# Two transformer blocks on one core: the FFNs' normed input made in three stages over three pairs of panels, and the split buffers at three distances mod 512 from the moving tiles

## The reference

```python
def rmsnorm(x, gain):
    y = xf * lax.rsqrt(jnp.mean(xf * xf, axis=-1, keepdims=True) + NORM_EPS_2)
    return (y * gain.astype(jnp.float32)).astype(x.dtype)

def modulate(h, shift, scale):
    return h * (1.0 + scale) + shift

def swiglu(u, wg, wu, wd):
    return (jax.nn.silu(u @ wg) * (u @ wu)) @ wd

    # in each layer l; the second FFN in the same way with mod 6, 7 and 8
    u = modulate(rmsnorm(h, norm_ffn1[l]), mod[:, :, 0], mod[:, :, 1])
    h = h + 0.5 * (1.0 + mod[:, :, 2]) * swiglu(u, ffn1_wg[l], ffn1_wu[l], ffn1_wd[l])
```

## Time and profile before

| | us |
|---|---|
| median of 3 runs | 1980.22 |
| lowest and highest | 1978.51 and 1980.4 |
| the profiled execution's own time | 1979.45 |
| its span, first to last instruction | 1978.1 |
| TensorE matmul busy | 1879.3 (95%) |
| VectorE busy | 1352.3 (68%) |
| ScalarE busy | 955.4 (48%) |
| DMA engines, mean rate | 197 GB/s |

### The profile page before, as it was taken

The page is one execution under the profiler, slowest core; times in us unless marked ns, Lnnn a source line. Parts: engine busy times, 40 slices in busy tenths (PEclk is TensorE's granted clock), DMA queues, the critical chain, the costliest instruction groups (busy, mean ns, idle before and its releaser), DMA issues.

```text
span 1978.1 us, 34269 instructions
## 1 busy us (share of the span) xinstructions
PE 1879.3 (95%) x15080; PEld 1811.9 (92%) x15080; DVE 1352.3 (68%) x1831; ACT 955.4 (48%) x1320; POOL 62.3 (3%) x76
## 2 busy tenths in 40 slices
PE   7998988899999888999999999999999999999998
PEld 7987988899788887999989899999999999799998
DVE  5666676665766767777676857777777776856555
ACT  5564554455645545444455335345434456344443
POOL 0000100000001000000000000001000000010000
PEclk9998999989989998999999999999999999999999
DMA  7453446463443554566545344665666456345551
GB/s 305 173 198 130 185 184 226 184 240 144 186 179 139 222 212 179 226 246 243 218 184 236 117 168 181 248 253 236 235 239 248 193 195 237 125 149 192 177 186 65
DMA packets 59285, 389.71 MB, mean 197 GB/s; under 512 B 6656, under 2 KB 9472, under 8 KB 15232
## 3 DMA queue, kind: packets, MB, share of 16 engines
q1 hardware_dynamic: 59136, 387.52, 51.1%
HBM read 386.45 MB, written 1.05 MB: 196 GB/s over the span
## 4 chain that ended last, share of the span: by engine, by line
PE 67%; DVE 21%; ACT 10%; issue 1%; DMA 0%; POOL 0%; SPq 0%; DVEq 0%; ACTq 0%
PE banks L757 17%; PE banks L758 16%; PE banks L759 16%; DVE weights_split L905 7%; ACT weights_split L899 4%; PE bank L758 4%; PE bank L757 4%; PE bank L759 4%; ACT map L1340 2%; DVE weights L885 1%; DVE xbc L2311 1%; DVE map_stat L1528 1%; ACT map L1346 1%; PE bank L825 1%; PE bank L838 1%
## 5 line engine op out<-in xcount | busy, mean ns | idle before, releaser
L905 DVE TENSOR_TENSOR weights_split<-weights,weights_split 128x2048 fp32r<-128x2048 f32 (+2 forms) x306 | 657.1, 2149 | 320.1 <-ACT weights_split L899 319.4
L757 PE MATMUL banks<-u,weights_split 128*128 128x258 f32 (+2 forms) x2032 | 583.3, 287 | 20.2 <-DVE weights_split L905 11.4
L899 ACT CAST weights_split<-weights 128x2048 fp32r<-128x2048 f32 (+2 forms) x306 | 542.9, 1776 | 77.0 <-PE bank L759 45.2
L758 PE MATMUL banks<-u,weights_split 128*128 128x258 f32 (+2 forms) x2032 | 577.8, 284 | 0.0
L759 PE MATMUL banks<-u,weights_split 128*128 128x258 f32 (+2 forms) x2032 | 577.7, 284 | 0.0
L757 PEld LDWEIGHTS banks<-u,weights_split 128*128 128x128 f32 (+1 forms) x2032 | 389.3, 192 | 24.7 <-DVE weights_split L905 12.4
L758 PEld LDWEIGHTS banks<-u,weights_split 128*128 128x128 f32 (+1 forms) x2032 | 389.2, 192 | 0.4
L759 PEld LDWEIGHTS banks<-u,weights_split 128*128 128x128 f32 (+1 forms) x2032 | 388.7, 191 | 0.4
L757 PE MATMUL banks<-x,weights_split 128*128 128x256 f32 x1056 | 302.4, 286 | 15.0 <-DVE weights_split L905 10.0
L758 PE MATMUL banks<-x,weights_split 128*128 128x256 f32 x1056 | 296.7, 281 | 0.0
L759 PE MATMUL banks<-x,weights_split 128*128 128x256 f32 x1056 | 296.6, 281 | 0.0
(11 more groups left out here) (320 smaller groups left out, 2519.6 us busy)
## 6 DMA issues: line engine op xcount, KB each, us to landing
weights<-in_weights SPq DMA_DIRECT2D x262, 1024.0 KB, 6.9
weights<-in_ada SPq DMA_DIRECT2D x80, 1024.0 KB, 4.8
weights<-in_weights SPq DMA_DIRECT2D x36, 512.0 KB, 5.4
weights<-in_weights SPq DMA_DIRECT2D x4, 576.0 KB, 5.3
constants_second<-in_constants_second SPq DMA_DIRECT2D x1, 1792.0 KB, 9.3
weights<-in_weights SPq DMA_DIRECT2D x2, 640.0 KB, 7.4
h<-in_x SPq DMA_DIRECT2D x2, 512.0 KB, 5.2
out<-xbc SPq DMA_DIRECT2D x4, 256.0 KB, 2.1
```

The costliest lines, as they stand in the source:

```text
L757: pe.matmul(out, left[0], right[0], start=start, stop=False, **more)
L758: pe.matmul(out, left[0], right[1], start=False, stop=False, **more)
L899: act.do.copy(split[:, 0, 0:n], raw[:, 0:n]).then_inc(*self.act_wrote.inc(("weights", key)))
L905: dve.do.tensor_tensor(split[:, 1, 0:n], raw[:, 0:n], split[:, 0, 0:n].bitcast(F32), ALU.subtract).then_inc(*self.dve_wrote.inc(("weights" ...
```

## The change

Pairs 0, 1 and 2 of each FFN (`RAWS = 3`) still use the raw input, which has a tile `raw` of its own now, with rows of 258 words. Meanwhile the normed input is made in `u`, whose rows are now 256 words: VectorE scales h by coefficient and factors into `squares`, ScalarE adds the shift and casts the high part into `u`, VectorE writes the low part. The step `normed` is issued six times, three times in pair 1 and three times in pair 2. At turn t VectorE scales chunks 2t and 2t+1, ScalarE makes the high parts of the two chunks before these, and VectorE the low parts of the two before those. Pairs 3 to 10 use `u`: 256 columns, one Silu of 512 wide from the bank on ScalarE, one multiplication of 512 wide from the bank on VectorE, with no scaling and no shift column. The modulations begin at pair 3 instead of pair 1. A spacer of 32 words stands behind each of the three split buffers instead of behind the last. Waits for the reuse of the raw tile and the factors name the third pair of the FFN before instead of its last.

```diff
@@ -60,13 +60,13 @@
...
 PAIRS = FC // 2
+RAWS = 3
 PLACES = HIDDEN_BLOCKS // 2
...
 SPLIT_SLOTS = 3
-U_ROW = 384
 AHEAD = 2
@@ -451,11 +451,19 @@
...
         self.add("accumulators", "ffn" + n, l)
-        self.mods_pause = False
+        self.pause_mods()
         for i in range(1, PAIRS + 1):
...
                 self.loads.append(("constants_second",))
-            if i < PAIRS:
+            if i == RAWS:
+                self.mods_pause = False
+            if i < RAWS:
+                self.normed(n, l, at, 3 * i - 3)
+                self.pair("wg" + n, l, i)
+                self.normed(n, l, at, 3 * i - 2)
+                self.pair("wu" + n, l, i)
+                self.normed(n, l, at, 3 * i - 1)
+            elif i < PAIRS:
                 self.pair("wg" + n, l, i)
@@ -463,6 +471,10 @@
...
             self.run(self.accumulate("wd" + n, l, i - 1))
+
+    def normed(self, n, l, at, turn):
+
+        self.add("normed", "ffn" + n, l, at, *[slice(max(2 * turn - k, 0), max(2 * turn - k + 2, 0)) for k in (0, 2, 4)])
@@ -671,8 +683,11 @@
...
         self.raw = self.new_ring([self.tile(f"weights{i}", [P, SLOT]) for i in range(RAW_SLOTS)])
-        self.split = self.new_ring([self.tile(f"weights_split{i}", [P, 2, SLOT], F32R) for i in range(SPLIT_SLOTS)])
-        self.tile("space", [P, 32])
+        split = []
+        for i in range(SPLIT_SLOTS):
+            split.append(self.tile(f"weights_split{i}", [P, 2, SLOT], F32R))
+            self.tile(f"space{i}", [P, 32])
+        self.split = self.new_ring(split)
         self.const = {"both": self.tile("constants", [P, columns(CONST_SIZES["both"])[1]])}
@@ -1653,9 +1668,9 @@
...
         b = self.b = {}
-        u = sb("u", [P, DC, 2, U_ROW], F32R)
-        b["u_shift"], b["u"] = u[:, :, :, 0:T + 2], u[:, :, :, 0:T]
+        b["u"] = sb("u", [P, DC, 2, T], F32R)
         b["y"] = sb("y2", [P, HIDDEN_BLOCKS, 2, T], F32R)
+        b["raw"] = sb("raw", [P, DC, 2, T + 2], F32R)
         b["square_sum"] = sb("square_sum", [P, 1, T])
@@ -1894,9 +1909,12 @@
...
-        pe, u, (hi, lo, _, _) = self.pe, self.b["u_shift"], self.panel(key)
+        pe, u, (hi, lo, _, _) = self.pe, self.b["raw"], self.panel(key)
         name, l, i = key
         tag = ("ffn" + name[-1], l)
+        if i >= RAWS:
+            self.tensor_normed_pair(key, j)
+            return
         if j == 0:
@@ -1917,6 +1935,22 @@
...
+    def tensor_normed_pair(self, key, j):
+
+        pe, u, (hi, lo, _, _) = self.pe, self.b["u"], self.panel(key)
+        tag = ("ffn" + key[0][-1], key[1])
+        if j == 0:
+            self.pairs.take(key)
+            pe.wait_ge(*self.pairs.free(key))
+            pe.wait_ge(self.dve_wrote, ("weights", key))
+        order, cols = self.chunk_order(tag[0]), slice(j * P, (j + 1) * P)
+        for c in order:
+            pe.wait_ge(self.dve_wrote, ("u", tag, c))
+            last = self.parts(self.pairs.tile(key)[:, j, 0:T], (hi[:, c, cols], lo[:, c, cols]),
+                              (u[:, c, 0, :], u[:, c, 1, :]), c == order[0], c == order[-1])
+        if j == 1:
+            last.then_inc(*self.filled.inc(("bank", key, 0), ("read", key)))
+
     def tensor_accumulate(self, key, half):
@@ -1956,11 +1990,13 @@
...
                 if before := self.tag_before(name, l):
-                    act.wait_ge(self.filled, ("read", ("wu" + before[0][-1], before[1], PAIRS - 1)))
+                    act.wait_ge(self.filled, ("read", ("wu" + before[0][-1], before[1], RAWS - 1)))
                 act.wait_ge(self.dve_wrote, ("coefficients", name, l))
-                self.scalar_hi(b["u_shift"][:, :, 0, T:T + 2], self.shifts(l, shift), ("shifts", (name, l)))
+                self.scalar_hi(b["raw"][:, :, 0, T:T + 2], self.shifts(l, shift), ("shifts", (name, l)))
             elif what == "raw":
                 self.scalar_raw(*at)
+            elif what == "normed":
+                self.scalar_normed(*at)
             elif what == "factors":
@@ -2075,16 +2111,16 @@
...
-        act, b, u, order = self.act, self.b, self.b["u_shift"], self.chunk_order(name)
+        act, b, raw, order = self.act, self.b, self.b["raw"], self.chunk_order(name)
         if name == "ffn2":
...
                 act.wait_ge(self.dve_wrote, ("h2", before, c))
-            if read := self.u_read(name, l, c):
-                act.wait_ge(self.filled, read)
+            if earlier := self.tag_before(name, l):
+                act.wait_ge(self.filled, ("read", ("wu" + earlier[0][-1], earlier[1], RAWS - 1)))
             act.wait_ge(self.dve_wrote, ("coefficients", name, l))
-            act.do.activation(u[:, c, 0, 0:T], self.h[:, c, :], ACT.Copy, scale=b["coef"][:, 0, c:c + 1]).then_inc(
+            act.do.activation(raw[:, c, 0, 0:T], self.h[:, c, :], ACT.Copy, scale=b["coef"][:, 0, c:c + 1]).then_inc(
                 *self.act_wrote.inc(("hi", ("raw", (name, l), c))))
@@ -2102,7 +2138,8 @@
...
         if before := self.tag_before(name, l):
-            act.wait_ge(self.dve_wrote, ("up_scaled", before, PAIRS - 1))
+            act.wait_ge(self.dve_wrote, ("up_scaled", before, RAWS - 1))
+            act.wait_ge(self.dve_wrote, ("scaled_u", before, self.chunk_order(before[0])[-1]))
         act.do.copy(self.b["factors"][:, 0:T], self.scores.tile(bank)[:, 0:T]).then_inc(
@@ -2110,8 +2147,16 @@
...
         tag, at = ("ffn" + name[-1], l), 2 * (i % PLACES)
+        if name.startswith("wg"):
+            self.hidden.take((tag, i))
         buf = self.hidden.tile((tag, i))
-        if name.startswith("wg"):
+        if name.startswith("wg") and i >= RAWS:
+            act.wait_ge(self.filled, ("bank", key, 0))
+            act.wait_ge(*self.hidden.free((tag, i)))
+            act.do.activation(buf[:, :, 0:T], self.pairs.tile(key)[:, :, 0:T], ACT.Silu).then_inc(
+                *self.act_wrote.inc(("bank", key, 0)))
+            self.pairs.emptied(key, self.act_wrote, ("bank", key, 0))
+        elif name.startswith("wg"):
             act.wait_ge(self.dve_wrote, ("gate_scaled", tag, i))
@@ -2121,6 +2166,17 @@
...
             self.scalar_hi(self.b["y"][:, at:at + 2, 0, :], buf[:, :, 0:T], ("hidden", tag, i))
+
+    def scalar_normed(self, name, l, at, _, high, __):
+
+        act, b, order = self.act, self.b, self.chunk_order(name)
+        for c in order[high]:
+            if read := self.u_read(name, l, c):
+                act.wait_ge(self.filled, read)
+            act.wait_ge(self.dve_wrote, ("scaled_u", (name, l), c))
+            act.do.activation(b["u"][:, c, 0, :], b["squares"][:, c, :], ACT.Identity,
+                              bias=self.mods[:, 72 * l + at + c:72 * l + at + c + 1]).then_inc(
+                *self.act_wrote.inc(("hi", ("u", (name, l), c))))
@@ -2168,12 +2224,14 @@
...
                 name, l, shift = at
-                u = b["u_shift"]
+                u = b["raw"]
                 dve.wait_ge(self.act_wrote, ("hi", ("shifts", (name, l))))
...
                 self.vector_raw(*at)
+            elif what == "normed":
+                self.vector_normed(*at)
             elif what == "first_gate":
@@ -2325,7 +2383,7 @@
...
-        dve, u, order = self.dve, self.b["u_shift"], self.chunk_order(name)
+        dve, u, order = self.dve, self.b["raw"], self.chunk_order(name)
         for i in range(DC + 1):
@@ -2340,10 +2398,13 @@
...
         tag, at = ("ffn" + name[-1], l), 2 * (i % PLACES)
+        if i >= RAWS:
+            self.vector_normed_pair(key)
+            return
         factors = self.heads(self.b["factors"][:, :], 1).to_broadcast([P, 2, T + 2])
...
         if name.startswith("wg"):
-            buf = self.hidden.take((tag, i))
+            buf = self.hidden.tile((tag, i))
             dve.wait_ge(self.filled, ("bank", key, 0))
@@ -2360,6 +2421,38 @@
...
                                         ALU.mult).then_inc(*self.dve_wrote.inc(*[("up", tag, i)] * j))
+        self.vector_lo(self.b["y"][:, at:at + 2, 1, :], buf[:, :, 0:T], self.b["y"][:, at:at + 2, 0, :],
+                       ("hidden", tag, i))
+        self.hidden.emptied((tag, i), self.dve_wrote, ("hidden", tag, i))
+
+    def vector_normed(self, name, l, at, scale, _, low):
+
+        dve, b, tag, order = self.dve, self.b, (name, l), self.chunk_order(name)
+        for c in order[scale]:
+            dve.wait_ge(self.act_wrote, ("factors", tag))
+            dve.wait_ge(self.pool_wrote, ("square_sum", tag))
+            dve.do.scalar_tensor_tensor(b["squares"][:, c, :], self.h[:, c, :], b["coef"][:, 0, c:c + 1],
+                                        b["factors"][:, 0:T], ALU.mult, ALU.mult).then_inc(
+                *self.dve_wrote.inc(("scaled_u", tag, c)))
+        for c in order[low]:
+            dve.wait_ge(self.act_wrote, ("hi", ("u", tag, c)))
+            dve.do.scalar_tensor_tensor(b["u"][:, c, 1, :], b["squares"][:, c, :],
+                                        self.mods[:, 72 * l + at + c:72 * l + at + c + 1],
```

(15 more changed lines are left out.)

## The result

The changed kernel takes 1955.65 us (median of 4 runs, 1952.25 to 1959.57), the kernel before 1979.37 (4 runs, 1975.82 to 1980.4). The ratio is 0.9881, 95% interval 0.9861 to 0.9901: 1.2% faster. The forecast was 1955.

The account below looks back on a forecast made before the run. PE, busy 95% of the span, was taken to bound the kernel through the spacing of matmul starts. From 1979.45 us, -22.8 + 2 + 0 - 4 = -24.8 gave 1954.7; with 0.8 added, 1955 us, range 1945 to 1974.

Parts of the forecast that it names:

- Pairs 3 to 10: Normed wg and wu matmuls go from 258 to 256 columns at the wd panels' pace, 113.4 ns: 22.8 us less.
- rival 4: Columns don't make the 120.8 ns; normed panels gain only 0.9 ns a matmul, time 1975 us; chance 0.05.
- The reason that I gave for the fast pace: The wd panel just before pair 3 has the fast pace, which has held through panel borders without a stop.
- Rival 1: The slow pace holds in the normed pairs: 1973 us, or 1980 with wd slow as well; chance 0.16.
- The split buffers: Different relations of the three buffers to x, u and y change PE's pace: 4 us less, ends 9.8 less and 7 more.
- twelve stretches outside the FFNs: Stretches without a stop at the slow pace, 270.65 us for some 2300 matmuls; at 113.3 ns they would be 260.8.
- The fast pace bears all four relations: Read from the 160-column panel, whose relation steps by 128 bytes at each chunk: 114.0 ns, handing on the fast pace.
- panels now fast turn slow: Bad end of the split buffers' part: after a stop, 1700 split matmuls outside the FFNs lose 4.4 ns each, 7 us more.
- The stages: Making the normed input in pairs 1 and 2: PE waits about 0.5 us in each FFN, 2 us more in all.
- Rival 2: The stages come late because casts slip a turn on DVE: 8 us instead of 2, time 1965; chance 0.07.
- The raw tile: Raw input in rows of 258 words, 1152 matmuls of pairs 0 to 2 stay at 120.8 ns: 0.
- Rival 3: Slower than before: the two moved split buffers, holding wu and wd panels, get a worse pace; +34, 1989 us; chance 0.08.

Follow-up runs that it names:

- e3: The changed kernel with matmuls of pairs 3 to 10 at 258 columns instead of 256; 1993.86 us, 1.0069 of the kernel before.
- e5: The changed kernel with 254, 248, 224 and 128 columns in the four FFNs' normed panels, first and last chunks excepted; 1967.13 us in one run.
- e1: The changed kernel with one 32-word spacer behind the third split buffer, all distances 192 bytes mod 512; 1962.05 us, 0.9906 of the kernel before.
- e6: The changed kernel with no spacer, all three split buffers at distance 64 bytes mod 512; 1980.61 us, 1.0007 of the kernel before.
- e11: The changed kernel with a single 64-word spacer behind the third split buffer, all distances 320; 1982.21 us, 1.0013 of the kernel before.
- e2: The kernel before with a 32-word spacer behind each split buffer and nothing else; 1985.32 us, 1.0029 of the kernel before.
- e12: The changed kernel with a single 96-word spacer behind the third split buffer, all distances 448; 1960.82 us, 0.9903 of the kernel before.
- e9: The changed kernel with four additional VectorE multiplications from PSUM in each normed pair, results unused; 2004.47 us, 1.0128 of the kernel before.
- e7: The changed kernel with three spacers of 16 words instead of 32, distances 256, 192, 128; 1988.99 us, 1.0052 of the kernel before.
- e13: The changed kernel without the spacer between second and third split buffer, distances 320, 192, 192; 1952.20 us, 0.9863 of the kernel before.

## Why the prediction was right

**Pairs 3 to 10: -22.8 forecast, -21.9 measured.** The pace that I read from the wd panels is the one that the normed panels got, less two slow stretches of pair 3 and wd 2 in the first FFNs. e3 shows that the columns make it. The Trainium skill's rule of the isolated gap ("TensorE: Matmul & The Clock Gate", "Back-to-back issue gap", N/2.4 plus 2.5 ns) gives an estimated 109 ns for 256 and 110 for 258 (the 2.6 us that I worked out from it are for all four blocks, not for one); measured were 113.3 and 121.6, so rival 4, which stood near it, was out. The Trainium skill says itself that the formula is for a single matmul and that both the weight load and the matmul set the spacing in a stream; the floor near 113 in e5 agrees with that.

**The reason that I gave for the fast pace was not enough.** I took it because the wd panel ahead was fast. It wasn't: with the spacers the wd panels of pairs 0 and 1 are slow (two panels of 5.65 in each FFN, against the earlier trace rows), and in the first FFNs pair 3 inherited that. Rival 1, the slow pace in the normed panels, is what e1 shows in both second FFNs, and e6 and e11 in all four. The three distances are what kept it out. So the sign and the size come from the columns, as forecast; that this part came out at its fast end, on a reason that did not hold, is luck: with one distance (e1) the blocks gave 13.0 us.

**The split buffers: -4 forecast, about -5 measured (0.9881 against 0.9906, the intervals overlap), in another place.** I had put it into twelve stretches outside the FFNs. By the traces 8.9 us lie in the blocks (532.47 to 523.56), and elsewhere there is some loss, as the runs differ by less. Outside the FFNs the slow pace did become rarer, the mean of the spacings under 140 ns went from 116.0 to 115.1 over some 6,700 matmuls. But e1, with one distance, has 115.0 there too, and its stages outside the FFNs are 6.4 us shorter than before, those of the changed kernel only 2.4 without the late panel. So in these executions nothing outside the FFNs is the spacers' gain. The step that failed is the one by which I gave the placement 4 us there, and a faster pace counts little where PE waits for others. "The fast pace bears all four relations" was too much as well: with a distance of 64 or 320 for all buffers all four FFNs are slow. And the end "panels now fast turn slow" came true for wd with 258 columns (e2). The Trainium skill's rule ("SBUF — State Buffer", "SBUF: two separate sides", PE waits for nobody on its port) would make this part 0. e6, e11 and e12 differ in nothing but the length of a spacer, and stand 20 us apart, so the rule doesn't cover what these runs show.

**The stages: +2 forecast, 0 measured.** The queue by hand was 1.1 us too late at the low part of wg 3, counted from the start of the panel (1.1 us ahead instead of 2.2), and 1.3 at the last low parts of u (2.8 after it instead of 1.5). Two neighbouring instructions of 256 columns take 0.87 to 0.88 us together and not 0.96, and casts went on beside them. The margin that is left is 0.66 us. Rival 2 was no nearer than that; e9 shows what the same queue costs when it is late.

**The raw tile: 0 forecast.** The raw panels of pairs 1 and 2 went from 120.8 ns to 119.4 to 120.2, some 0.8 us less in all, and their eight wd panels gave back 1.6.

**The sum.** -21.9 in the blocks, -2.4 outside the FFNs, -2.4 in one raw stage of layer 1 where before the granted clock of one panel had been 0.78, +5.7 for the late panel and +1.2 in what is left (the 0.8 and 1.6 of the part above, and 0.4 after the last FFN) make the -19.8 between the two spans; without the late panel it is -25.5, where I had -24.8. That the medians came within 1 us of the forecast is in part luck: the stages were 2 us better than counted, the blocks 0.9 worse, and the clock's 2.4 us stood in no term. Rival 3 didn't come: no buffer has a pace of its own in the changed kernel. e7 shows that it could have, at other distances.

## What to carry to other kernels

Read a matmul's cost from the spacing of starts in whole panels, for each width on its own: here 240 and 256 columns cost the same and 258 cost 8 ns more, so two additional columns were worth a rearrangement of three engines. Where one panel has two paces in a trace, the addresses belong to the things to vary: try several distances between weights and moving operand, together with the rest of the change, as the same spacers were worth -5 us with it and +6 without. And the slack of an engine is in the margin of its queue's next due result, not in its busy share; a result that frees a buffer for a load counts among them.

## What was unexpected of the hardware

- Two paces of float32r matmuls of 256 columns, 113.3 and 117.8 ns at granted clock 1.00, each held for up to 1152 matmuls. With one distance mod 256 between weights and moving rows the pace that came stayed (192) or was slow in all FFNs (64). A step from 64 to 192 between two panels ended the slow one, in e13 at wd 2 in four of four FFNs, but not behind raw panels (wd 0 and wd 1 in e13), and in the changed kernel at wg 3 in only two FFNs, in the others one round later. A stop of PE could start it (e9). What in the memory or the engine does this is open.
- 258 to 274 columns cost 121.6 to 126.7 ns, 240 and 256 columns 113.3, and 128 columns 112.8. Panels of 254 columns ran at 117.9, which may be the slow pace.
- With distances of 256, 192 and 128 bytes (e7) two panels of three were slower than either pace: 119.3 ns on average.
